# Marking the closing branch of TensorE's expert loop as one that goes back to the head

## The reference

```python
def expert_block(args):
    xblk, e = args
    gu = xblk @ w_gu[e] + b_gu[e]
    gate = jnp.minimum(gu[:, ::2], SWIGLU_LIMIT)
    up = jnp.clip(gu[:, 1::2], -SWIGLU_LIMIT, SWIGLU_LIMIT)
    act = (up + 1.0) * gate * jax.nn.sigmoid(SWIGLU_ALPHA * gate)
    return act @ w_down[e] + b_down[e]

yb = lax.map(expert_block, (xb, block_e))
y = yb.reshape(-1, D)[dest] * gate_sorted[:, None]
return jnp.zeros_like(h).at[tok_sorted].add(y)
```

## Time and profile before

| | |
|---|---|
| median of three runs | 2677.33 us (2676.52 to 2683.94) |
| the profiled execution | 2674.82 us, span 2673.0 us |
| PE busy | 2431.1 us, 91% of the span |
| PEld busy | 2153.8 us, 81% |
| DVE busy | 1805.6 us, 68% |
| ACT busy | 1556.7 us, 58% |
| POOL busy | 808.7 us, 30% |
| granted TensorE clock, mean | 0.97 |

### The profile page before, as it was taken

One profiled execution on the slowest core, in us unless ns is written; L12 is line 12 of the kernel. 1 busy time (PEld: TensorE's weight loads), 2 busy tenths in 40 slices (PEclk: granted clock), 3 DMA queues, 4 the chain that ended last, 5 costly groups with the idle time before them and its releaser, 6 DMA issues. The chain is left out here.

```text
span 2673.0 us, 135770 instructions
## 1 busy us (share of the span) xinstructions
PE 2431.1 (91%) x57165; PEld 2153.8 (81%) x57165; DVE 1805.6 (68%) x2119; ACT 1556.7 (58%) x1972; POOL 808.7 (30%) x638
## 2 busy tenths in 40 slices
PE   6999998999988759999899989988889999999993
PEld 2455558999984449989898989988888999999993
DVE  3786986666657772552818377777877686788883
ACT  4524544555555352553737467777776676677873
POOL 3222116767731121221212232222222222223230
PEclk9999998999999869999999999999999999999996
DMA  8621001101122283572919397889988797899965
GB/s 286 242 77 62 1 16 35 31 24 31 31 91 80 95 331 95 170 258 56 372 33 371 121 337 261 309 315 345 334 300 315 283 321 253 285 330 369 330 244 195
DMA packets 123432, 536.91 MB, mean 201 GB/s; under 512 B 12236, under 2 KB 12608, under 8 KB 90560
## 3 DMA queue, kind: packets, MB, share of 16 engines
q1 hardware_dynamic: 107120, 481.80, 48.2%
q0 software_dynamic: 14880, 48.91, 8.2%
q10 hardware_dynamic: 1360, 5.24, 0.5%
HBM read 496.99 MB, written 38.92 MB: 200 GB/s over the span
## 5 line engine op out<-in xcount | busy, mean ns | idle before, releaser
L2523 PE MATMUL ps<-qkv,weights 128*128 128x64 f16 x10496 | 938.2, 193 | 68.0 <-DVE weights L1937 34.1
L2523 PEld LDWEIGHTS ps<-qkv,weights 128*128 128x128 f16 x10496 | 922.0, 98 | 85.4 <-DVE weights L1937 40.0
L2525 PE MATMUL ps<-qkv,weights 128*128 128x64 f16 x10496 | 937.8, 193 | 4.9 <-issue 4.9
L2524 PE MATMUL ps<-qkv,weights 128*128 128x64 f16 x10496 | 937.8, 193 | 0.1
L2525 PEld LDWEIGHTS ps<-qkv,weights 128*128 128x128 f16 x10496 | 922.5, 98 | 2.4 <-issue 2.4
L2524 PEld LDWEIGHTS ps<-qkv,weights 128*128 128x128 f16 x10496 | 922.5, 98 | 0.2 <-issue 0.2
L1937 DVE SCALAR_TENSOR_TENSOR weights<-hT,weights 128x2048 f16<-128x2048 f16 (+1 forms) x256 | 587.8, 2346 | 167.4 <-ACT weights L1320 138.1
L1320 ACT ACTIVATE weights<-hT 128x2048 f16 (+1 forms) x256 | 527.1, 2101 | 87.1 <-DMA hT<-in_w_gu_dram 65.4
L2540 PE MATMUL ps<-qkv,weights 128*128 128x64 f16 x5248 | 472.8, 193 | 24.6 <-DVE weights L1942 22.3
L2540 PEld LDWEIGHTS ps<-qkv,weights 128*128 128x128 f16 x5248 | 461.7, 98 | 32.3 <-DVE weights L1942 27.9
L2541 PE MATMUL ps<-qkv,weights 128*128 128x64 f16 x5248 | 472.5, 193 | 0.0
(11 more groups left out here) (450 smaller groups left out, 4308.2 us busy)
## 6 DMA issues: line engine op xcount, KB each, us to landing
hT<-in_w_gu_dram SPq DMA_DIRECT2D x256, 1024.0 KB, 8.6
qkv<-in_w_down_dram SPq DMA_DIRECT2D x128, 1024.0 KB, 6.2
weights<-in_w_ada_dram SPq DMA_DIRECT2D x8, 2048.0 KB, 14.4
qkv<-in_w_in_dram SPq DMA_DIRECT2D x4, 2048.0 KB, 9.0
qkv<-in_w_ada_dram SPq DMA_DIRECT2D x4, 2048.0 KB, 8.7
hT<-decay_rows SPq DMA_DIRECT2D x20, 256.0 KB, 3.3
hT<-beta_rows SPq DMA_DIRECT2D x20, 256.0 KB, 3.3
qkv<-in_x_dram ACTq DMA_DIRECT2D x4, 1024.0 KB, 8.1
```

Source lines behind the costliest of these rows:

```text
L2523: pe.matmul(dst, ghi[k][:, b, c], xT[:, 0, k, :], start=first, stop=False, skip_group_check=True)
L2524: pe.matmul(dst, ghi[k][:, b, c], xT[:, 1, k, :], start=False, stop=False, skip_group_check=True)
L2525: last = pe.matmul(dst, glo[k][:, b, c], xT[:, 0, k, :], start=False, stop=end, skip_group_check=True)
```

## The change

The loop of PE is opened with `nc.Fori` for PE's engine alone and with `hint_back_edge=True`. This puts one instruction more at the very head of the loop's body, ahead of the `If`: it names the compare-and-branch that closes the loop and says that it will go to the head. It is executed in each of the 95 turns, those that skip their body among them. The loop's counter, its bound, its body and the other engines' loops are as they were, and `If` branches carry no such mark.

```diff
             pe.sem_inc(s_dn, DK)
             pe.sem_inc(s_ty, 1)
-            with pe.Fori(0, MAXB) as t:
+            with nc.Fori(0, MAXB, engines=(pe.engine,), hint_back_edge=True) as t:
                 with pe.If(t <= nlast):
                     for k in range(GK):
                         gate_up(t, k)
```

## The result

The changed kernel takes 2685.84 us in the median of 17 runs (2674.2 to 2697.79), the kernel before 2677.54 us in 17 runs (2672.04 to 2684.9). The ratio is 1.0031, with a 95% interval of [1.0019, 1.0042]: 8.3 us slower, 5.1 to 11.2. That is a real loss, and it lies right at the 0.3% that I had set as the bound of "no change". My own sign of being wrong, a median that moves by over 8 us, is met, if only by 0.3 us. The range of 2673 to 2690 us holds the result; the 3.2 us of the forecast are too small by more than half.

The account below looks back on a forecast made before the run. PE, busy 91% of the span, was taken to bound the kernel. 64 heads on the path x 0.05 us = 3.2 us on the 2677.33 us median gave 2680.5 us, range 2673 to 2690 us.

Parts of the forecast that it names:

- My own sign of being wrong: Median moves by over 8 us, or stays while the turn's edge has moved by more than 0.1 us.
- No fetch to save: At the loop's turn edges no instructions are brought in, 0 packets in 81 edges, so the mark saves no fetch.
- rival A: Mark shortens the turn's edge, by a saved fetch or quicker branch: 2653 us, or 2672 us for a third; chance 7%.
- Rival B: Mark brings the head's instructions in again each turn, 0.95 us a packet, 61 us in all: 2738 us; chance 5%.
- D: Mark does nothing that is seen, under queued matmuls or in the noise: 2677 us; chance 13%.
- The price of a mark: One added sequencer instruction on PE at the head of each turn costs 0.05 us.
- How many heads count: At most 31 of 82 marks hidden by weight waits; at least 51, with 13 skipped turns 64, on the path.
- The skipped turns: At the loop's end, 13 skipped turns all count at 0.05 us each; gap grows from 9.54 to 10.2 us.
- The exit: Behind the loop, the wrong mark in the 95th turn may cost one packet, 0.95 us; in the range, not the sum.
- rival C: Mark at the head costs the dearest step seen, 0.18 us: 11.5 us at 64 heads, 17 at 95; chance 10%.

Follow-up runs that it names:

- late: Kernel before with the mark placed 72 matmuls ahead of the end of down, none at the head; ratio 0.9999 to the kernel before.
- again2: The changed kernel a third time, one mark at the head, on a chip where the kernel before was traced too; ratio 1.0036 to the kernel before.
- control: The kernel before, unchanged, without a mark, timed against itself and traced once more; ratio 1.0006.
- disarmed: Kernel before plus the mark at the head, its outcome read from a register holding 'not taken', so it names no target; ratio 1.0019, 5.1 us slower.
- five: Kernel before with five marks at the head, all for the same closing branch; ratio 1.0091 to the kernel before, 24.2 us slower.
- boundmark: Kernel before with PE's loop ending at nlast + 1 instead of 95, `If` kept, mark at the head; ratio 0.9991 to the kernel before.
- middle: Kernel before with the mark behind gate and up, ahead of the 16 transposes, none at the head; ratio 1.0014 to the kernel before, 3.7 us slower.
- before: First trace of the kernel before, without a mark; profiled execution 2674.82 us, median 2677.54 us in 17 runs.
- noif: Kernel before with PE's loop ending at nlast + 1 and its `If` removed, no mark; ratio 0.9974 to the kernel before, 6.9 us faster.
- bound: Kernel before with only PE's loop end set to nlast + 1 instead of 95, `If` kept, no mark; ratio 0.9982, 4.8 us faster.
- allbound: Kernel before with all five engines' loops ending at the last block and PE's `If` gone, no mark; ratio 0.9945, 14.7 us faster.
- again3: The changed kernel, traced a fourth time, on another chip; ratio 1.0023 to the kernel before, 6.2 us slower.

## Why the prediction came out as it did

**No fetch to save: right.** The instruction queues are empty in the loop with and without the mark, and the edge of `late` is no shorter than the one before. By this the Trainium skill's figure of 2048 instructions for PE's memory ("Runtime: NRT & Kernel Launch", section "Instruction fetch mechanics") holds for this loop, and its sentence on a two-page window doesn't; rival A with it is refuted. Rival B is refuted by the same empty queues, and D, under which nothing would be seen, by the edge.

**The price of a mark: too low by half.** I took 0.05 us from the difference between two kinds of edges. Measured: 0.10 to 0.11 us at an edge, with one mark and with five, and 0.12 us in a skipped turn; a turn of one expert takes 18.86 us in `again2` and 18.75 in `control`. `disarmed` shows that it is the step itself at the edge. The difference of 0.04 us was the nearest row in size, but it was not a row of an instruction. I had said that no row of before shows the price. That holds for the views, but the trace keeps records of PE's sequencer that no view prints. In the skipped turns of `control` a register step is followed by the next instruction after 0.09 to 0.10 us, and a taken branch after 0.27 to 0.31 us; in `again2` a mark is followed by the next after 0.09 us, and the two taken branches of the turn take 0.22 to 0.23 us instead of 0.21 to 0.22. So a mark costs what any plain step costs, and with it in force the taken branches are slower by 0.01 to 0.02 us; `disarmed` has the 0.09 us without the slower branches.

**How many heads count: too many with five marks, open with one.** I let the turns with new weights swallow at most 31 of 82 marks. `five` shows that 39 to 55 are swallowed. The reason that I gave, the transfer started in the turn before, fits: in the five-mark trace the waits for DVE fall as "issue" rises. But the count by turns with new weights was no upper bound; that a turn ahead of the change of weights is swallowed with it is likely, but not shown. For one mark the four timings have a mean of 8.3 us, which less 1.5 and 2.2 us for the end of the loop leaves 4.6 us, or 44 heads, between the 35 and my 51. With 35 heads the price and the count err in opposite directions: 35 x 0.105 = 3.7 us, where I had 51 x 0.05 = 2.6 us. So that these terms come near each other is in part luck.

**The skipped turns: right in kind, 0.65 us forecast, 1.5 us measured.** All 13 count in full.

**The exit: left out of the sum, and it is a third of the loss.** I named it with 0.95 us in the range. In the four traces of the changed kernel it is a pause of 1.8 to 2.4 us from matmul to matmul, and it lies on the chain. This is the chain of waits of `again2` at the end of the loop, for the earlier trace rows:

```profile
2616.74 8.80 issue
2625.55 1.89 PE ps L2550 x8
2627.54 2.20 issue
```

Only kernels whose last closing branch was marked have it (the changed kernel in four traces, `boundmark`, and with 0.90 us `five`); `disarmed`, `middle` and `late` don't. The packets of q8 tell why. In all 14 traces they number seven around the loop: five at the entry and two at the exit in the seven without a mark in force by the end of the first turn (`before`, `control`, `disarmed`, `late`, `noif`, `bound`, `allbound`), four and three in the other seven. So without a mark one packet comes in at the entry, some 4 us after the loop's first closing branch, and stays for the whole loop; with a mark it comes only when the loop is left. In the six traces with the pause PE goes on 1.3 to 1.5 us after the end of this packet. In `middle` it moves under the skipped turns, where nobody waits for it. That it holds the code behind the branch is inferred from this; no record names what a packet holds.

The price stood in the trace before too. In the loop's first turn, while q8 moves its packets of the entry, PE stands still under "issue" in the middle of gate and up:

```profile
986.54 0.20 PE L2525 MATMUL ps<-qkv,weights 128*128 128x64 f16 x1 [2.27 <-issue]
```

A packet of q8 ends 1.48 us ahead of this row, and the same happens at 993.36 us, with 2.65 us of idle time and 1.59 us. The 0.95 us of the earlier trace rows is what a packet takes on its queue; PE stands still for more than twice that. Why the pause of `five` is only 0.90 us stays open: its packet starts 0.5 us after the first L2550 behind the loop, and in the other five traces 1.2 to 1.6 us after it.

The sum as measured, with the heads by `five`: 3.7 (heads) + 1.5 (skipped turns) + 2.2 (exit) = 7.4 us. The four timings of this kernel gave 8.3 (5.1 to 11.2), 9.1 (5.3 to 13.1), 9.6 (5.9 to 13.3) and 6.2 us (3.2 to 8.8). For `disarmed`: 35 x 0.10 + 1.0 = 4.5 us, measured 5.1. The mechanism was the forecast's, nothing to save and a step added on the path; the size lies between the forecast (3.2 us) and rival C (11.5 us at 64 heads), to which I gave 10%. The upper end of the range, which holds the measured median, came from rival C, not from the terms of my forecast.

**What I read wrongly afterwards.** From the first trace of the changed kernel I took the pauses in the middle of turns for an effect of the mark, with 18 us in the loop that would have explained everything. One repeat of the changed kernel without them, and `bound`, which has them and no mark, undid this. Traces with them also have shorter waits for DVE's L1937: 21.7 and 25.6 us in the two of the changed kernel with pauses (the first and `again3`), 31.0 and 30.2 us in the two without. So the first trace shows more swallowing than a single mark brings about.

## What to carry to other kernels

Before marking a loop's branch, look whether the instruction queues move anything while the loop runs. Here they have no row there, and the mark had nothing to save: it cost 0.10 us at a turn's edge, and some 2 us at the exit, because a packet that otherwise came in at the entry came in there. For the price of a packet take a place where the engine stood still for one, not the packet's own time. A sequencer's step is paid where the engine has nothing queued, at a turn's edge or in an empty turn, and cost nothing measurable in the middle of a run of matmuls. The same steps offer a gain when they are taken away: a loop that ends at the run's own count, without an `If` in it, is worth 0.26% here on PE alone (`noif`), and 0.55% when all engines have it (`allbound`).

## What the hardware showed that was not expected

- PE paused for 0.2 to 0.4 us in the middle of matmul runs in every trace of one chip (four kernels, two of them without a mark, some 70 to 80 pauses each, most of them 130 to 145 matmuls into a turn, or 40 to 95 matmuls into `down`) and in none of eight traces of two others. In the timings of that chip the kernel before is slower by 16 to 18 us (2679.52 against 2663.42 and 2661.47 us); whether the pauses are the reason is not shown, and their cause is open. One trace of a kernel with a new feature isn't enough to blame the feature for what is new in it.
- A mark in force makes a skipped turn dearer by 0.12 us, one that names nothing by 0.08 us.
